# Two transformer blocks on one core: stacks of the even attention made earlier, first norm's squares added on VectorE, norm sums taken inside the last output tile

## Chip, cores, metric

One core of a Trainium2 chip runs the whole program in one launch. The metric is the device time in microseconds (us), lower is better. TensorE is called PE in the profile, VectorE DVE, ScalarE ACT, GpSimd POOL, and SyncE (which here only issues transfers) SP.

## The reference

Input x has 512 tokens of width 1024, the context 256 tokens. A first block of two layers modulates, mixes and projects; a second block of two layers adds attention, a gated unit and two feed-forward nets. Cut to what the change touches:

```python
def rms_norm(x, g):
    y = xf * lax.rsqrt(jnp.mean(xf * xf, axis=-1, keepdims=True) + EPS)
    return (y * g)

# first_block, layer l
mod_x = (silu_c @ w_mod[l] + b_mod[l])
sh_x, sc_x, g_x = jnp.split(mod_x, 3, axis=-1)
hx = rms_norm(x, norm_pre[l]) * (1.0 + sc_x) + sh_x       # the same for ctx
px = hx @ w_in
mx = mixer(px, pc)
x = x + g_x * rms_norm(mx @ w_out[l], norm_post[l])

# second_block, layer i
h = rms_norm_2(x, norm_mix_pre[i]); h = attention(h) or chunked_sgu(h)
x = x + rms_norm_2(h, norm_mix_post[i])
h = conv_gated_ffn(rms_norm_2(x, norm_ffn_pre[i]))
x = x + rms_norm_2(h, norm_ffn_post[i])
```

So there are twelve norms over the 1024 features: one before and one after each mixer or net.

## The kernel before

Features lie on the 128 partitions in KT = 8 tiles, tokens along the free axis (TX = 512 of x, TC = 256 of the context, TA both). All engines run their own hand-written order of instructions and meet through counting semaphores. There is no scheduler, so the code's order is the order of the work.

**Weights.** Every float32 matrix is read as panels of 1 MB (`load`, on SyncE) into a ring of RING = 3 slots `raw`. VectorE turns each into two float32r parts (`split_at`: a cast to `whi`, a subtraction to `wlo`, which takes raw's place). TensorE multiplies hi*hi, hi*lo and lo*hi (`mm3`, lines 385 to 387). `panel_done` frees the slot for the load three panels later.

**Start.** SyncE issues parameters, x, context and constants (`mats`), then the twelve modulation panels of layer 0 in six loads of 2 MB (`load_mod0`), among them the first two panels of the even phase. ScalarE squares one tile at a time (`square("pre0", kt)`), and TensorE sums each tile over its partitions by multiplying with a column of ones (`column_sums`, line 506, for pre0 and pre1 tile by tile: `sums_by_tile`). After that come the root (ScalarE, `norm_root`), its reciprocal (VectorE, `norm_inverse`) and its spread over the partitions (TensorE, `spread`, line 531). TensorE makes the modulation rows (`mod_panel`, line 490), ScalarE copies them out (`mod_row`), TensorE turns them into columns (`mod_columns`, line 499). VectorE then normalises x tile by tile (`pre_norm`), and the first panel of the even phase follows at its pace (`paced_panel`).

**Even attention.** 48 units: four pairs of heads (hp), six query tiles (t), two heads (a). For each pair, a stack of operands (query and key parts side by side on partitions) is made: ScalarE casts (`even_hi`), VectorE subtracts (`even_lo`, line 1786), and SyncE issues 24 small transfers in a row (`build_stack`, lines 349 to 351). The next pair's cast stands at unit (t, a) = (1, 1) of a pair, its subtraction at (2, 0). TensorE computes scores two units ahead (`even_scores`, line 630), which at a pair's first unit waits for the stack. VectorE takes maxima (line 1834) and mixes the two softmaxes (line 1852).

**Norms behind and ahead of panels.** For the ten other norms VectorE adds the squares of tiles 0 to 6 (`add_square`, line 1632), and `sums_added` on TensorE multiplies with ones twice: the sum `acc`, then the last square `sq[1]`. After an output projection (out0, out1, wo, the "long" ffn_out and sgu_out) this follows the last panel. For a norm ahead of a net (mixpre, ffnpre) the scale per token is applied after the matmul: `paced_pair` runs the first two panels, `sums_added` follows, then the third panel, then `spread`, after which ScalarE copies the spread root to `rxs` and VectorE scales the panels (`q_scaled`, `ff["scaled"]`), which frees their PSUM banks for the fourth panel.

Of the kernel before, what the change touches and what calls it, by code (L numbers as in the profile page):

```python
# [36 lines left out]
KT = D // P  # L37
# [51 lines left out]
def build_kernel(nc, dram, out):  # L89
    with ExitStack() as ctx:  # L90
# [145 lines left out]
        BY_TILE = {"pre0": 0, "pre1": 1}  # L236
        ADDED = {k: i for i, k in enumerate(k for k in NORMS if k not in BY_TILE)}
        ADDS = KT - 2

# [10 lines left out]
        n_full = {k: sem(f"{k}_full") for k in BY_TILE}  # L250
# [129 lines left out]
        def _(pe):  # L380
# [128 lines left out]

            def sums_by_tile(key, tiles):  # L510
# [233 lines left out]
            def out_projection(phase, norm, hi, lo, parts_made, kts=range(KT)):  # L744
                p0 = FIRST[phase]
                for k in range(4):
# [4 lines left out]
                    if k == 0:  # L751
                        paced_panel(p0, (0, 1), None, hi, lo, parts_made, kts)
                    else:
                        feature_panel(p0 + k, (2 * s, 2 * s + 1), None, hi, lo, kts)
# [15 lines left out]
            sums_added("post0")  # L770
# [173 lines left out]
            feature_panel(p0 + 3, (3, 4), None, o1hi, o1lo, kts1)  # L944
            pe.wait_ge(y_free, Y_AT["out1"] + 2)
            sums_added("post1")
# [86 lines left out]
            sums_added("mixpost0")  # L1033
# [1366 lines left out]
```

## Time and profile before

| | before |
|---|---|
| median of 3 runs | 2368.78 us (2367.3 to 2369.19) |
| the profiled execution's own time | 2371.67 us |
| its span, first to last instruction | 2369.9 us |
| PE / DVE / ACT busy | 2218.5 / 1345.8 / 545.0 us |
| granted TensorE clock, mean | 0.960 |

The profiled execution took 2.9 us more than the median. Its span leaves 1.8 us around it. Busy TensorE time counts matmuls, whose ends are modelled.

### The profile page before, as it was taken

The page shows a single profiled execution, that of the slowest core. Times are in us where ns is not written, and L with a number is a line of the kernel's source. Part 1 is how long each engine was busy: PE and PEld are TensorE (multiplying, and loading weights), DVE is VectorE, ACT ScalarE, POOL GpSimd, SP SyncE. Part 2 cuts the span into 40 slices and gives each one's busy share as a digit, 9 for nine tenths or more (in the row PEclk, how much of TensorE's full clock was granted, in tenths as well). Part 3 has the DMA queues.
Part 4 walks back from the last instruction along what each step waited for, and adds up shares of the span by engine and source line. Part 5 has one row for each costly group of instructions (what it writes and reads, how often), then busy time and mean ns, then how long its engine had stood idle before and what let it go on. Part 6 is the DMA issues. An engine that isn't in the chain of part 4 may idle for free.

```text
span 2369.9 us, 28220 instructions
## 1 busy us (share of the span) xinstructions
PE 2218.5 (94%) x11900; PEld 1819.0 (77%) x11900; DVE 1345.8 (57%) x1727; ACT 545.0 (23%) x1071; POOL 46.3 (2%) x31
## 2 busy tenths in 40 slices
PE   6999997779999989889899999999999999999997
PEld 5788885448878767777788888878888787788886
DVE  2323436884464264668578773464687436877633
ACT  2111014771231263246311111021100002211100
POOL 0000000000001020110000000000000000000000
PEclk9899998898899999899899999999999999999998
DMA  8022223121122110211223222322221222223222
GB/s 360 19 107 107 107 108 76 45 59 39 69 71 99 39 68 28 84 50 37 71 90 106 89 90 94 105 86 89 89 89 63 91 96 89 89 90 106 79 98 72
DMA packets 35246, 203.99 MB, mean 86 GB/s; under 512 B 4912, under 2 KB 5168, under 8 KB 17200
## 3 DMA queue, kind: packets, MB, share of 16 engines
q1 hardware_dynamic: 33744, 197.47, 24.1%
q10 hardware_dynamic: 1376, 4.72, 0.6%
q8 instruction: 94, 1.54, 0.3%
q14 instruction: 32, 0.26, 0.0%
HBM read 190.64 MB, written 2.10 MB: 81 GB/s over the span
## 4 chain that ended last, share of the span: by engine, by line
PE 86%; DVE 8%; SPq 2%; ACT 2%; issue 1%; DMA 1%; DVEq 0%; POOL 0%; POOLq 0%; ACTq 0%
PE ps L385 22%; PE ps L386 22%; PE ps L387 21%; PE ps L458 3%; PE ps L459 3%; PE ps L460 3%; PE ps L506 2%; PE ps L550 1%; DVE stat L1834 1%; PE ps L490 1%; PE ps L630 1%; PE ps L1120 1%; PE ps L531 1%; PE ps L851 1%; SPq L349 1%
## 5 line engine op out<-in xcount | busy, mean ns | idle before, releaser
L1623 DVE CAST whi<-raw 128x2048 fp32r<-128x2048 f32 (+2 forms) x162 | 184.4, 1138 | 485.7 <-DMA raw<-in_ffn_out 117.4
L385 PE MATMUL ps<-h2hi,whi 128*128 128x512 f32 x1040 | 410.2, 394 | 18.6 <-DVE h2lo L1720 12.2
L386 PE MATMUL ps<-h2lo,whi 128*128 128x512 f32 x1040 | 407.8, 392 | 0.0
L387 PE MATMUL ps<-h2hi,wlo 128*128 128x512 f32 x1040 | 407.6, 392 | 0.0
L1624 DVE TENSOR_TENSOR wlo<-raw,whi 128x2048 fp32r<-128x2048 f32 (+2 forms) x162 | 341.6, 2108 | 5.6
L385 PE MATMUL ps<-h1hi,whi 128*128 128x512 f32 (+1 forms) x768 | 274.5, 357 | 9.5 <-DVE h1lo L1665 8.3
L386 PE MATMUL ps<-h1lo,whi 128*128 128x512 f32 (+1 forms) x768 | 270.1, 352 | 0.0
L387 PE MATMUL ps<-h1hi,wlo 128*128 128x512 f32 (+1 forms) x768 | 268.2, 349 | 0.0
L385 PEld LDWEIGHTS ps<-h2hi,whi 128*128 128x128 f32 x1040 | 197.3, 190 | 61.1 <-issue 13.3
L387 PEld LDWEIGHTS ps<-h2hi,wlo 128*128 128x128 f32 x1040 | 197.1, 189 | 41.3
L386 PEld LDWEIGHTS ps<-h2lo,whi 128*128 128x128 f32 x1040 | 197.3, 190 | 40.6
L385 PE MATMUL ps<-mhi,whi 128*128 128x512 f32 x544 | 212.6, 391 | 6.6 <-DVE mlo L1643 3.9
L387 PE MATMUL ps<-mhi,wlo 128*128 128x512 f32 x544 | 212.4, 390 | 0.0
L386 PE MATMUL ps<-mlo,whi 128*128 128x512 f32 x544 | 212.3, 390 | 0.0
L385 PEld LDWEIGHTS ps<-h1hi,whi 128*128 128x128 f32 x768 | 147.8, 192 | 34.8 <-issue 10.4
L386 PEld LDWEIGHTS ps<-h1lo,whi 128*128 128x128 f32 x768 | 147.7, 192 | 19.8 <-issue 1.4
L387 PEld LDWEIGHTS ps<-h1hi,wlo 128*128 128x128 f32 x768 | 146.9, 191 | 19.9
L385 PEld LDWEIGHTS ps<-mhi,whi 128*128 128x128 f32 x544 | 102.5, 188 | 29.1 <-issue 4.3
L1144 ACT ACTIVATE temp<-ps 128x512 f32<-128x512 f32 (+1 forms) x48 | 25.5, 564 | 429.4 <-PE ps L387 413.6
L387 PEld LDWEIGHTS ps<-mhi,wlo 128*128 128x128 f32 x544 | 102.4, 188 | 21.4
L386 PEld LDWEIGHTS ps<-mlo,whi 128*128 128x128 f32 x544 | 102.5, 188 | 21.2
L2130 DVE TENSOR_TENSOR temp<-ps,rxs 128x1024 f32<-128x1024 f32 x44 | 53.9, 1224 | 89.3 <-PE ps L387 74.5
(284 smaller groups left out, 2993.9 us busy)
## 6 DMA issues: line engine op xcount, KB each, us to landing
raw<-in_ffn_in SPq DMA_DIRECT2D x44, 1024.0 KB, 4.9
raw<-in_ffn_out SPq DMA_DIRECT2D x32, 704.0 KB, 4.0
raw<-in_even SPq DMA_DIRECT2D x16, 1024.0 KB, 7.0
mod_w<-in_mod SPq DMA_DIRECT2D x6, 2048.0 KB, 26.0
mraw<-in_mod SPq DMA_DIRECT2D x12, 1024.0 KB, 4.9
raw<-in_odd SPq DMA_DIRECT2D x12, 1024.0 KB, 5.0
raw<-in_sgu_v SPq DMA_DIRECT2D x12, 1024.0 KB, 4.9
raw<-in_sgu_u SPq DMA_DIRECT2D x12, 1024.0 KB, 5.1
```

The lines of the kernel that those rows point to most:

```text
L349: sp.dma_start(q[to, :].bitcast(F32), (qhi, eql[:, hp, :])[part][rows, :].bitcast(F32)).then_inc(ea["stack"], 16)
L385: pe.matmul(o, r(lhi), r(rhi), start=first, stop=False, **kw)
L386: pe.matmul(o, r(lhi), r(rlo), start=False, stop=False, **kw)
L387: return pe.matmul(o, r(llo), r(rhi), start=False, stop=last, **kw)
L458: pe.matmul(o, lhi, rhi, start=kt == 0, stop=False)
L459: pe.matmul(o, lhi, rlo, start=False, stop=False)
L460: return pe.matmul(o, llo, rhi, start=False, stop=kt == KT - 1)
L506: done = pe.matmul(ps[:, 6, 48 + t:49 + t], tile[:, t * P:(t + 1) * P], ones[:, 0:1], start=first and t == tiles[0], stop=last, skip_group ...
L1144: return act.activation(o, in_, func, **kw)
L1623: step(dve.tensor_copy(whi[:, slot, 0:width].bitcast(F32R), raw[:, slot, 0:width]))
L1624: tell(dve.tensor_tensor(wlo[:, slot, 0:width].bitcast(F32R), raw[:, slot, 0:width], whi[:, slot, 0:width], ALU.subtract), split_done, n + 1)
L2130: tell(dve.tensor_tensor(gu[s], ps[:, b:b + 2, :], rxs[:].unsqueeze(1).broadcast_to([P, 2, TX]), ALU.mult), ff["scaled"], c0 + n + 1)
```

## The change

The diff touches four places.

1. Start: `mats` is loaded before x, and the even phase's first two panels go between the modulation loads. pre0's squares (x and context, 768 columns) are added on VectorE, and TensorE sums the total once, after the second modulation panel. `spread("pre0")` stands after the fifth. The second even panel's cast moves to ScalarE, at tile 4 of the first norm, and its subtraction behind that norm.
2. Even attention: the next pair's cast is made at unit (0, 0), the subtraction at (0, 1).
3. Norms ahead of nets: VectorE adds the eighth square too, TensorE sums only `acc` (`pre_sums`). `spread` goes between the two halves of the third panel (not so for mixpre1, where it stays).
4. Norms behind projections: the sum over `acc` is put into the last tile (`last_out_panel`, `long_out`), with only the last square's sum left behind it. In out1 and wo ScalarE can square tile 6 when the last panel's first half is done. VectorE's adds go ahead of the splits beside them.

In this diff the edit at mixpre0 stands for ffnpre0 and ffnpre1 too, `last_sums(norm)` with the test of (t, half) is in `long_out`, `cast_ahead` in ScalarE's `hi_parts`, and the last piece in `out_splits`.

```diff
             sp.dma_start(pc[:], dram["params"]).then_inc(params_in, 16)
+            sp.dma_start(mats[:], dram["mats"]).then_inc(params_in, 16)
             sp.dma_start(x[:], dram["xT"]).then_inc(x_in, 16)
             sp.dma_start(cx[:], dram["ctxT"]).then_inc(x_in, 16)
-            sp.dma_start(mats[:], dram["mats"]).then_inc(params_in, 16)
...
-            for i in range(4):
-                load_mod0(i)
-            for k in range(2):
-                load("even", k, k)
+            load_mod0(0)
+            load_mod0(1)
+            load("even", 0, 0)
+            load_mod0(2)
+            load_mod0(3)
+            load("even", 1, 1)
...
+            def last_out_panel(n, banks, hi, lo, norm, kts=range(KT)):
+                pe.wait_ge(split_done, n + 1)
+                for j in range(2):
+                    for i, kt in enumerate(kts):
+                        if (j, i) == (1, 4):
+                            acc_sums(norm)
+                        last = x_part(n, banks[j], j, kt, hi, lo, i == 0, i == KT - 1)
+                    if j == 0:
+                        last.then_inc(out_half, 1)
+                last.then_inc(panel_done, 1)
...
-            def sums_added(key):
-                pe.wait_ge(n_acc, ADDS * ADDED[key] + ADDS)
+            def acc_sums(key):
+                pe.wait_ge(n_acc, ADD_AT[key] + ADDS)
                 column_sums(acc, range(4), True, False)
+            def last_sums(key):
                 pe.wait_ge(n_sq, KT * NORM[key] + KT)
                 column_sums(sq[1], range(4), False, True).then_inc(n_mm, 1)
+            def pre_sums(key, tiles=range(4)):
+                pe.wait_ge(n_acc, ADD_AT[key] + KT - 1)
+                column_sums(acc, tiles, True, True).then_inc(n_mm, 1)
...
-            sums_by_tile("pre0", range(6))
-            mod_panel(0, 0)
-            spread("pre0", range(6))
             for k in range(8):
-                if k:
-                    mod_panel(0, k)
+                mod_panel(0, k)
+                if k == 2:
+                    pe.wait_ge(n_rt, 1)
                 if k:
                     mod_columns(0, k - 1)
+                if k == 1:
+                    pre_sums("pre0", range(6))
+                elif k == 4:
+                    spread("pre0", range(6))
...
-            sums_added("mixpre0")
-            feature_panel(p0 + 2, (4, 5), None, h2hi, h2lo)
-            spread("mixpre0", range(4))
+            pre_sums("mixpre0")
+            feature_panel(p0 + 2, (4, 5), None, h2hi, h2lo, between=lambda: spread("mixpre0", range(4)))
...
+                        if (t, half) == (KT - 1, 1):
+                            acc_sums(norm)
...
-                sums_added(norm)
+                last_sums(norm)
...
+                    if ctx_too and kt == 4:
+                        act.wait_ge(raw_loaded[1], 16)
+                        copy(whi[:, 1, :].bitcast(F32R), raw[:, 1, :]).then_inc(cast_ahead, 1)
...
-                if (t, a) == (1, 1) and hp < 3:
+                if (t, a) == (0, 0) and hp < 3:
                     even_hi(hp + 1)
...
-                if (t, a) == (2, 0) and hp < 3:
+                if (t, a) == (0, 1) and hp < 3:
                     even_lo(hp + 1)
...
+            for kt in range(1, KT):
+                add_square("pre0", kt, TA)
             norm_inverse("pre0", 6)
-            for n in range(2):
-                split_at(n)
+            split_at(0)
...
-                add_square(key, 6)
+                for kt in (4, 5, 6):
+                    add_square(key, kt)
+                split_at(p0 + 5)
```

On TensorE, at the program's start, the instructions stood so (L506 sums over partitions, L490 a modulation panel, L499 its columns, L531 the spread root):

```order
L506 MATMUL ps<-mats,temp 128x1 x48
L490 MATMUL ps<-mod_w_74,cs 32x256 x8
L531 MATMUL ps<-mats,root 128x128 x6
L490 MATMUL ps<-mod_w_74,cs 32x256 x8
L499 MATMUL ps<-pc,rows 128x2 x2
```

They now stand so (the same functions, at lines 511, 495, 504 and 556):

```order
L495 MATMUL ps<-mod_w_74,cs 32x256 x16
L504 MATMUL ps<-pc,rows 128x2 x2
L511 MATMUL ps<-mats,temp 128x1 x6
L495 MATMUL ps<-mod_w_74,cs 32x256 x8
L504 MATMUL ps<-pc,rows 128x2 x2
L495 MATMUL ps<-mod_w_74,cs 32x256 x8
L504 MATMUL ps<-pc,rows 128x2 x2
L495 MATMUL ps<-mod_w_74,cs 32x256 x8
L504 MATMUL ps<-pc,rows 128x2 x2
L556 MATMUL ps<-mats,root 128x128 x6
```

48 products with ones became 6, and the modulation panels no longer stand behind them.

On VectorE, in the first pair of the even attention, the subtraction (L1786) stood after the maximum (L1834) that follows unit 4's mix (L1852):

```order
L1852 SCALAR_TENSOR_TENSOR prob_87<-prob_87,stat 128x768
L1834 TENSOR_REDUCE stat<-ps 128x2
L1786 TENSOR_TENSOR eql<-eq,eql 128x768
L1786 TENSOR_TENSOR ekl<-ek,ekl 128x768
L1848 RECIPROCAL stat<-stat 128x1
L1849 SCALAR_TENSOR_TENSOR stat<-stat,lam 128x1
L1852 SCALAR_TENSOR_TENSOR temp<-temp,stat 128x768
```

It now stands three units earlier, behind unit 1 (maximum L1876, mix L1894, subtraction L1828):

```order
L1890 RECIPROCAL stat<-stat 128x1
L1891 SCALAR_TENSOR_TENSOR stat<-stat,lam 128x1
L1894 SCALAR_TENSOR_TENSOR prob_87<-prob_87,stat 128x768
L1876 TENSOR_REDUCE stat<-ps 128x2
L1828 TENSOR_TENSOR eql<-eq,eql 128x768
L1828 TENSOR_TENSOR ekl<-ek,ekl 128x768
```

The same instructions are there as before, so the work of a pair on VectorE is unchanged, and only SyncE's start on the next stack moves.

## Rows read from the trace of the kernel before

**Rows 1.** Waits of TensorE, whole span: total us, times, longest.

```profile
PE ps L630 <- DMA esb<-ekl: 17.5, 3, 6.2
```

**Rows 2.** Timeline of the first 60 us: start, duration, engine, line, count, idle.

```profile
14.72 1.28 ACT L1208 ACT_TABLE_LOAD   x1
16.02 0.42 ACT L1144 ACTIVATE temp<-ctx 128x256 f32<-128x256 f32 x1
16.46 0.63 ACT L1144 ACTIVATE temp<-x 128x512 f32<-128x512 f32 x1
...
17.24 20.61 PE L506 MATMUL ps<-mats,temp 128*128 128x1 f32 x96 [17.24 <-ACT temp L1144]
...
37.78 1.93 PE L490 MATMUL ps<-mod_w,cs 128*32 128x256 f32 x16
...
42.35 1.07 PE L490 MATMUL ps<-mod_w,cs 128*32 128x256 f32 x16
...
54.57 0.38 DVE L1749 TENSOR_TENSOR modc<-ps,pc 128x16 f32<-128x16 f32 x2 [8.92 <-PE ps L499]
...
59.14 0.77 PE L385 MATMUL ps<-h1hi,whi 128*128 128x512 f32 x1 [4.68 <-DVE h1lo L1665]
```

**Rows 3.** Timeline of 97 to 112 us, modulation panels 8 to 11, one row.

```profile
105.09 1.01 PE L499 MATMUL ps<-pc,rows 128*128 128x2 f32 x4 [0.50 <-ACT rows L1144]
```

**Rows 4.** Loads issued at 1.70, 4.38 and 5.92 us: KB, us to landing.

```profile
ctx<-in_ctxT SPq DMA_DIRECT2D x1, 1024.0 KB, 10.3
...
mod_w<-in_mod SPq DMA_DIRECT2D x1, 2048.0 KB, 28.1
...
raw<-in_even SPq DMA_DIRECT2D x1, 1024.0 KB, 31.6
```

**Rows 5.** Timeline of even attention, VectorE and the DMA queue of SyncE.

```profile
397.36 0.95 DVE L1786 TENSOR_TENSOR eql<-eq,eql 128x768 fp32r<-128x768 f32 x1
...
399.21 0.51 SPq L349 DMA_DIRECT2D whi<-eql  x1
...
414.64 0.59 SPq L351 DMA_DIRECT2D esb<-ekl  x1
...
418.56 1.76 DVE L1834 TENSOR_REDUCE stat<-ps 128x2 f32<-128x1536 f32 x1 [5.71 <-PE ps L630]
...
459.92 1.76 DVE L1834 TENSOR_REDUCE stat<-ps 128x2 f32<-128x1536 f32 x1 [2.38 <-PE ps L630]
...
501.29 1.76 DVE L1834 TENSOR_REDUCE stat<-ps 128x2 f32<-128x1536 f32 x1 [5.22 <-PE ps L630]
```

**Rows 6.** Timeline after two pre norms: qkv (995 on) and ffn0_in (1190 on).

```profile
998.15 2.37 DVE L1624 TENSOR_TENSOR wlo<-raw,whi 128x2048 fp32r<-128x2048 f32 x1
...
1003.36 1.84 PE L506 MATMUL ps<-mats,temp 128*128 128x1 f32 x16
...
1008.41 2.29 DVE L1624 TENSOR_TENSOR wlo<-raw,whi 128x2048 fp32r<-128x2048 f32 x1
...
1016.08 1.05 PE L531 MATMUL ps<-mats,root 128*128 128x128 f32 x8
...
1019.41 0.50 PE L385 MATMUL ps<-h2hi,whi 128*128 128x512 f32 x1 [2.29 <-DVE sq L2038]
...
1209.82 0.50 PE L385 MATMUL ps<-h2hi,whi 128*128 128x512 f32 x1 [2.06 <-DVE temp L2130]
```

**Rows 7.** Timeline at the ends of out1, wo and ffn0_out.

```profile
969.62 2.69 PE L506 MATMUL ps<-mats,temp 128*128 128x1 f32 x16 [1.57 <-DVE temp L1632]
972.35 0.27 ACT L1144 ACTIVATE root<-ps,eps 128x4 f32<-128x4 f32 x1 [2.27 <-PE ps L506]
...
1162.52 0.27 ACT L1144 ACTIVATE root<-ps,eps 128x4 f32<-128x4 f32 x1 [1.26 <-PE ps L506]
...
1538.33 0.60 ACT L1144 ACTIVATE temp<-ps 128x512 f32<-128x512 f32 x1 [13.88 <-PE ps L387]
...
1540.07 0.26 ACT L1144 ACTIVATE root<-ps,eps 128x4 f32<-128x4 f32 x1 [0.66 <-PE ps L506]
```

More of the change, by code:

```diff
@@ L235, in build_kernel @@
         NORM = {k: i for i, k in enumerate(NORMS)}
-        BY_TILE = {"pre0": 0, "pre1": 1}
-        ADDED = {k: i for i, k in enumerate(k for k in NORMS if k not in BY_TILE)}
+        BY_TILE = {"pre1": 0}
         ADDS = KT - 2
+        ADDED = {k: 0 if k == "pre1" else KT - 1 if "pre" in k else ADDS for k in NORMS}
+        ADD_AT = {k: sum(ADDED[j] for j in NORMS[:i]) for i, k in enumerate(NORMS)}
         n_sq = sem("norm_squares")
@@ L249, in build_kernel @@
         out0_x = sem("out0_last_x")
-        n_full = {k: sem(f"{k}_full") for k in BY_TILE}
+        out_half = sem("out_last_half")
+        cast_ahead = sem("second_panel_cast")
+        n_full = {k: sem(f"{k}_full") for k in ("pre0", "pre1")}
         n_hi = {k: sem(f"{k}_hi") for k in NORMS if "pre" in k}
@@ L752, in out_projection @@
                         paced_panel(p0, (0, 1), None, hi, lo, parts_made, kts)
+                    elif k < 3:
+                        feature_panel(p0 + k, (2 * s, 2 * s + 1), None, hi, lo, kts)
                     else:
-                        feature_panel(p0 + k, (2 * s, 2 * s + 1), None, hi, lo, kts)
+                        last_out_panel(p0 + k, (2 * s, 2 * s + 1), hi, lo, norm, kts)
             pe.wait_ge(y_free, Y_AT["out0"] + 1)
@@ L769, in _ @@
                 ctx_part(p0 + 3, 5, 0, kt, h1hi, h1lo, i == 0, i == KT - 1)
-            sums_added("post0")
+            acc_sums("post0")
+            last_sums("post0")
             for i, kt in enumerate(kts0):
@@ L943, in _ @@
             pe.wait_ge(n_sq, KT * NORM["post1"] + 2)
-            feature_panel(p0 + 3, (3, 4), None, o1hi, o1lo, kts1)
+            last_out_panel(p0 + 3, (3, 4), o1hi, o1lo, "post1", kts1)
             pe.wait_ge(y_free, Y_AT["out1"] + 2)
-            sums_added("post1")
+            last_sums("post1")
             spread("post1", range(4))
@@ L1038, in ffn @@
                 paced_pair(p0, h2hi, h2lo, n_ok[f"ffnpre{layer}"])
-                sums_added(f"ffnpre{layer}")
-                feature_panel(p0 + 2, (4, 5), None, h2hi, h2lo)
-                spread(f"ffnpre{layer}", range(4))
+                pre_sums(f"ffnpre{layer}")
+                feature_panel(p0 + 2, (4, 5), None, h2hi, h2lo,
+                              between=lambda: spread(f"ffnpre{layer}", range(4)))
                 for n in range(3, 22):
@@ L1210, in _ @@
                 if kt >= 2:
-                    act.wait_ge(n_tile, kt - 1)
+                    act.wait_ge(n_acc, ADD_AT["pre0"] + max(1, kt - 2))
                 step(copy(sq[kt % 2][:, TX:TA], cx[:, kt, :], ACT.Square))
                 square("pre0", kt, x[:, kt, :])
-            norm_root("pre0", range(6))
             for k in range(8):
                 mod_row(0, k)
+                if k == 1:
+                    norm_root("pre0", range(6))
             hi_parts("pre0", h1hi, 0, True)
@@ L1341, in out_copy @@
                     n, b = FIRST[phase] + k, banks[k]
-                    act.wait_ge(panel_done, n + 1)
                     for j in range(2):
+                        if k == 3 and j == 0:
+                            act.wait_ge(out_half, 1 if phase == "out1" else 2)
+                        else:
+                            act.wait_ge(panel_done, n + 1)
                         kw = dict(bias=par(bias, 2 * k + j)) if bias else {}
@@ L1631, in add_square @@
                 a, b = (sq[0], sq[1]) if kt == 1 else (acc, sq[kt % 2])
-                tell(dve.tensor_tensor(acc[:, 0:TX], a[:, 0:TX], b[:, 0:TX], ALU.add), n_acc, ADDS * ADDED[key] + kt)
+                tell(dve.tensor_tensor(acc[:, 0:n_tok], a[:, 0:n_tok], b[:, 0:n_tok], ALU.add), n_acc, ADD_AT[key] + kt)
             def add_ctx_square(i, kt):
@@ L1733, in post_then_scaled @@
                 low(KT - 1)
+                add_square(pre, KT - 1)
             step(dve.memset(eps[:], EPS))
@@ L1765, in _ @@
                      lambda kt, c: modc[0][:, kt, c:c + 1])
+            dve.wait_ge(cast_ahead, 1)
+            tell(dve.tensor_tensor(wlo[:, 1, :].bitcast(F32R), raw[:, 1, :], whi[:, 1, :], ALU.subtract), split_done, 2)
             for n in range(2, 4):
@@ L2011, in out_splits @@
                 p0 = FIRST[phase]
-                for k in range(4):
+                for k in range(3):
                     split_at(p0 + k + 2)
-                    for kt in ((), (1,), (2, 3), (4, 5))[k]:
+                    for kt in ((), (1,), (2, 3))[k]:
                         add_square(key, kt)
-                add_square(key, 6)
+                for kt in (4, 5, 6):
+                    add_square(key, kt)
+                split_at(p0 + 5)
             out_splits("out1", "post1")
```

10 lines of the change are left out of this document (5 added, 5 removed).

## The prediction, made blind

> **What bounds the kernel now.** I read the page's busy times first: TensorE is busy for 2218.5 us of a span of 2369.9 (the table above), so what counts is the 150 us in which it is not, and the time in which it does work that could be left out. The waits of TensorE name one large releaser among the stages that the diff touches: three waits for the stacks' transfers, 17.5 us [rows 1]. The timeline of the start shows 17.24 us of nothing and then 20.61 us of sums over partitions, before the modulation's first panel at 37.78 [rows 2]. The rest of the change touches small gaps, each read from its timeline [rows 6, 7].
>
> **1. The start.** Now: the squares begin at 16.02, the 96 rows of sums (48 products, two rows each) take 20.61 us, 0.215 a row, the panels end so that VectorE can start the modulation at 54.57, and the paced panel starts at 59.14 [rows 2]. All this is one chain, so what the last modulation column gains, the kernel gains. New chain: x and context have landed at about 12.7 (the context came at 1.70 + 10.3 = 12.0 with `mats` behind it [rows 4]; the bytes ahead are now the same). The table load of 1.28 follows, so squares start at 14.0, not 16.02. A tile costs ScalarE 0.42 + 0.63, and VectorE an add of 768 columns, which is priced by the 0.95 us of a subtraction of that width [rows 2, 5]. Both run side by side, 1.07 a tile: squares end at 22.5, adds at 23.5. ScalarE's first row copy stands behind the squares, so panel 1 can only start at 22.9. It takes 1.93 at the lower clock level [rows 2] and ends at 24.8. Columns of 1.01 follow [rows 3], to 25.8, and then 6 products (12 rows of 0.215), to 28.4. An iteration of panel and columns without a gap costs 2.9 at this level: three of them (k = 2, 3, 4) end at 37.1. The spread takes 2.7 (42.35 - 37.78 - 1.93 [rows 2]), to 39.8. Panel 5 ends at 41.7. Panels 6 and 7 need the fourth modulation load. It landed at 4.38 + 28.1 = 32.5 and now has 1 MB ahead of it. Two MB took 37.5 - 32.5 = 5.0 us (to the second even panel, at 5.92 + 31.6) [rows 4], so it lands at 35.0 and is not waited for.
>
> What remains depends on the clock. The granted clock reads full in these stretches, but the same 16 panel rows take 1.93 at 37.78 and 1.07 at 42.35 [rows 2]: the first is the 1.2 GHz level, the second 2.4. The 20 us of one-column sums did not raise it. The panel of 1.93 and the spread after it, back to back, did. In the new order spread and panel 5 are the same pair of neighbours, so I take the upper level from 41.7 on: an iteration then costs (54.57 - 42.35) / 7 = 1.75 [rows 2], two of them with the leftover columns 4.7. The end is at 46.4, a gain of 54.57 - 46.4 = **8.2**. Bounds: all at the lower level, 41.7 + 1.0 + 2 x 2.9 + 1.0 = 49.5, gain 5.1; the upper level from panel 2 on, about 41, gain 13.5. I take the middle because panels 8 to 11, separated by gaps of 0.50, stayed at the lower level [rows 3].
>
> The Trainium skill ("TensorE: Matmul & The Clock Gate", Part 1) says that the throttled clock is the default and that sustained activity releases it. This speaks against the change, which empties TensorE's first 20 us, and would give 5.1 in place of 8.2, a sum of 28.2, if the loop does not count as sustained. The trace agrees only in part: the busy time taken away did not raise the clock.
>
> The cast that moved to ScalarE: 128x256 takes 0.42 and 128x512 0.63 [rows 2], so 2048 columns cost 0.42 + 7 x 0.21 = 1.9, and four times 0.63 = 2.5 at most. VectorE's pace in the norm is two products and two subtractions of x and context a tile, ScalarE's only two casts, so a delay of 2 us is taken up by a tile of lead. Value: nothing; uncovered 1 us. Panel 1's subtraction (below 2.37 [rows 6]) goes behind the norm, where TensorE still has the last tile and eight context products to do. Value: nothing; uncovered 2 us.
>
> **2. The stacks.** The subtraction at 397.36 is followed by 24 issues from 399.21 to 414.64, and the last lands 2 us later. Scores start then, and VectorE's maximum at 418.56 after 5.71 us idle. The other two boundaries cost VectorE 2.38 and 5.22 [rows 5]. TensorE's waits add to 17.5, but VectorE is what the units run at, so its idle time is the price: 13.3 in all. The second is smaller because a weight split of VectorE fills the wait. With the subtraction three units of some 3 us earlier, the stack is there 9 us earlier, against waits of at most 6.2 [rows 1]. ScalarE's cast and VectorE's two subtractions are the same work in another unit. SyncE's wait for the scores of the pair before holds for pair 2 and 3, but those are done one pair earlier. Gain **13.3**. Bounds: 10 if cast and subtraction at a boundary uncover 1 us each time; 16.5 if the short idles around the boundaries go too.
>
> **3. Sums ahead of nets.** Four norms lose half of their 16 rows (1.84 a norm, so 0.85 to 0.92 [rows 6]): **3.4**. VectorE's extra add (under 0.95) delays the third panel's split, which ended at 998.15 + 2.37 = 1000.5, while TensorE comes to it at 1005.2 [rows 6]: hidden by 4 us. Uncovered it would cost 0.7 each.
>
> **4. The spread in mid-panel.** After the spread TensorE waited 2.29 us for the first scaling at qkv and 2.06 at ffn0_in [rows 6], and ffn1_in has the same code. Spread, root copy and scaling took from 1016.08 to 1019.4, 3.4 us. Half a panel is 5.5 us ((1016.08 - 1005.1) / 2). So all three waits go: **6.4**. Bounds: 0 if the split of the fourth panel, which stands ahead of the scaling on VectorE, ended later than the panel; in the trace it ended at 1008.41 + 2.29 = 1010.7, before 1016.08 [rows 6]. I take 6.4, and 4 as the low end.
>
> **5. Sums behind projections.** In out1 the sums began 1.57 us after the last matmul, ran cold for 2.69, and the root came at 972.35 [rows 7]. New: 0.85 more in the tile, one square instead of two and no add behind it, 8 rows: the root at about 970.6, gain 1.7. In wo two biased copies stand between the last square and the root on ScalarE, which was idle for only 1.26 before the root at 1162.52. Square and copies now start 0.85 later less one square of 0.6, so 1.0 could come through; I take 0.85 [rows 7]. In the long ones there is nothing to gain: the first 8 rows ran in the shadow of the last square (1538.33, 0.60), and the root came at 1540.07 [rows 7]. Put into the tile, they lengthen it by 0.85 and the root comes at 1540.9. Three of these: -2.5. Sum **0.0**; from -2 to +1.5. Out0 has its sums where it had them.
>
> **Sum.** 8.2 + 13.3 + 3.4 + 6.4 + 0.0 = 31.3. The profiled execution's 2371.67 (span 2369.9 and 1.8 around it) would become 2340.4. It lay 2.9 above the median, so the median of 2368.78 becomes **2337.5**.
>
> **Rivals.**
> - *The clock stays low through the start.* Gain 28, time 2340.5. For it: panels 8 to 11 [rows 3]. The page of the Trainium skill named above, "TensorE: Matmul & The Clock Gate", would give this one. Against it: panel and spread raised it once.
> - *The upper level comes early in the loop.* Gain 36.5, time 2332. For it: there are no gaps in the new loop. Against: two thirds of it is panel work.
> - *ScalarE or TensorE becomes the bound at pair boundaries*, so that only half of the stacks' gain arrives. Gain 24.5, time 2344. For it: ScalarE gets 1.6 us of casts just where scores, maxima and exps of heavy units follow light ones. Against: VectorE is the one without gaps around 397 to 405.
> - *The stacks don't come earlier*, since SyncE issues them behind something else. Gain 18, time 2351. Against: each stack's other conditions are met before the cast.
> - *Slower than before.* TensorE enters the even panels from an emptier start. If the paced panel (a tile each 2.4 us) does not bring the upper level and the full panels behind it stay at 1.2 GHz, each costs its own length more: 11.0 for x [rows 6] and half of that for the context, 16.5. From the second such panel on, the 31 us are gone: 2370 with two, 2387 with three. For it: the kernel starts with less work. Against: the paced panel starts after 4.68 us of idleness now too [rows 2] and rose within it.
>
> **Chances.** Forecast 0.55 (its own range 2333 to 2341), clock low 0.18, clock early 0.09, half the stacks 0.11, no stacks 0.03, slower 0.02, and 0.02 for something that leaves no change. The range 2330 to 2345 leaves out the last three, and part of the others' tails. Faster by over 0.2% (about 5 us, what a measurement of this kernel can tell from no change): 0.96; within 0.2%: 0.02; slower: 0.02.
>
> **What would show it.** Modulation columns ending near 46 instead of 54.5, with 16 panel rows going from 1.93 to 1.07 after the spread. No wait of TensorE for the stacks, and no idle time of VectorE over 1 us at boundaries; the stage from the first maximum to the last unit shorter by 13. Eight rows of sums, not 16, and no wait for the first scaling in qkv and both ffn_in. Roots of the long projections 0.8 later after the tile's last but one matmul. Wrong would make it: a wait for `norm_added` inside a last tile, a wait of panel 1 for its split, a fourth panel that waits for its own split.

## The result, and the profile after

The changed kernel runs in **2327.46 us** (median of four runs, 2325.4 to 2330.14) against 2368.16 us for the kernel before (four runs, 2367.3 to 2369.19): ratio 0.9829, 95% interval 0.9812 to 0.9846. It is faster by 40.7 us, where the prediction said 31.3 and put the lower end of its range at 2330. The direction and three of the four parts came as forecast; the size is 9 us off, and what follows is mainly about these 9 us.

The profiled execution took 2330.14 us, span 2328.4. The start first: TensorE's timeline of the changed kernel (start, duration, operation, count, idle time before with its releaser), which answers to [rows 2].

```profile
25.49 1.93 PE L495 MATMUL ps<-mod_w,cs 128*32 128x256 f32 x16 [4.26 <-ACT rows L1175]
27.36 1.01 PE L504 MATMUL ps<-pc,rows 128*128 128x2 f32 x4
28.23 2.70 PE L511 MATMUL ps<-mats,temp 128*128 128x1 f32 x12
...
39.21 2.91 PE L556 MATMUL ps<-mats,root 128*128 128x128 f32 x12
42.05 1.84 PE L495 MATMUL ps<-mod_w,cs 128*32 128x256 f32 x16
43.81 0.61 PE L504 MATMUL ps<-pc,rows 128*128 128x2 f32 x4
44.49 1.07 PE L495 MATMUL ps<-mod_w,cs 128*32 128x256 f32 x16
...
52.99 0.77 PE L390 MATMUL ps<-h1hi,whi 128*128 128x512 f32 x1 [4.67 <-DVE h1lo L1703]
```

The loop has no gaps, the 96 rows of sums are 12, and the level rose where the forecast put it: panel 5 at 42.05 still took 1.84, panel 6 took 1.07. VectorE began the modulation at 48.42 instead of 54.57, 6.15 earlier and not 8.2. The missing 2 us lie ahead of the loop, in ScalarE's timeline:

```profile
14.20 1.28 ACT L1242 ACT_TABLE_LOAD   x1 [7.39 <-DMA ctx<-in_ctxT]
15.49 0.42 ACT L1175 ACTIVATE temp<-ctx 128x256 f32<-128x256 f32 x1
...
18.66 0.42 ACT L1175 ACTIVATE temp<-ctx 128x256 f32<-128x256 f32 x1 [1.12 <-DVE temp L1670]
```

The context landed at 14.2, not at 12.7 as worked out from [rows 4]; squares began at 15.49, not 14.0. Another 1.1 us went at the third tile, where ScalarE waited for VectorE's first add; the forecast had both run side by side without a wait. So panel 1 began at 25.49, not 22.9. The landing is the execution's and not the edit's: in the nine profiles of kernels that have this start, with the table load behind the wait for the context, that load began between 12.33 and 14.48 us (fill_norms and front_alone, both below), and in start_alone at 12.50.

In the attention, the queue's and VectorE's timelines answer to [rows 5]. The second pair's 24 issues went out between these two rows:

```profile
381.95 0.51 SPq L354 DMA_DIRECT2D whi<-eql  x1
...
397.35 0.59 SPq L356 DMA_DIRECT2D esb<-ekl  x1
```

and the first maximum of the heavy units behind them had waited 0.18 us, for a matmul, where it had waited 5.71 for the stack:

```profile
410.67 1.76 DVE L1876 TENSOR_REDUCE stat<-ps 128x2 f32<-128x1536 f32 x1 [0.18 <-PE ps L657]
```

TensorE's waits name no stack any more (17.5 us in [rows 1]). The lead grows from 6.03 to 20.17 us over the attention: 14.1 for a forecast of 13.3.

Behind out1 the changed kernel's TensorE shows sums, spread, the pre norm's sums and the spread in mid-panel (before: [rows 6, 7]):

```profile
940.37 0.95 PE L511 MATMUL ps<-mats,temp 128*128 128x1 f32 x8
...
944.97 1.02 PE L511 MATMUL ps<-mats,temp 128*128 128x1 f32 x8 [0.78 <-ACT temp L1175]
946.63 1.16 PE L556 MATMUL ps<-mats,root 128*128 128x128 f32 x8 [0.64 <-DVE root L1686]
...
975.19 0.95 PE L511 MATMUL ps<-mats,temp 128*128 128x1 f32 x8
...
981.57 1.05 PE L556 MATMUL ps<-mats,root 128*128 128x128 f32 x8
982.37 0.48 PE L390 MATMUL ps<-h2hi,whi 128*128 128x512 f32 x1
```

The wait of 2.29 for the first scaling is gone. But two rows are shorter than the change made them. The spread is the same eight rows as before and took 1.16, not 2.08 (972.95 in the trace of before), and from it to the pre norm's sums it is 28.56 us (946.63 to 975.19), not 30.41 (972.95 to 1003.36), though TensorE's work between them was not edited. The granted clock from the spread to the sums was 0.88, against 0.81 before.

Lead by stage, in the two profiled executions: start 6.0; attention +14.1; out0 and pre1, where nothing was edited, +4.2; out1's root +1.9; its paced pair +2.8; the sums and spread of qkv +2.6; wo with ffn0_in +6.2; ffn0_out, mixpre1 and sgu +0.1; sgu_out with ffn1_in +3.6; ffn1_out -0.9. So the excess over the forecast is 4.2 in a stage that is not edited, some 6 in the norms from out1 on and 0.8 in the attention, less 2 at the start.

### The profile page after: what moved, and what is told of

Its sections match the earlier page's. It is cut to its first block, busy times and chain, and to the rows that moved or that the text cites. A ratio compares the mean times of both kernels' runs of the same rounds, so it can differ in the third digit from the quotient of the medians.

```text
span 2328.4 us, 28021 instructions
## 1 busy us (share of the span) xinstructions
PE 2192.0 (94%) x11784; PEld 1790.3 (77%) x11784; DVE 1354.2 (58%) x1737; ACT 546.2 (23%) x1072; POOL 47.6 (2%) x31
## 4 chain that ended last, share of the span: by engine, by line
PE 86%; DVE 9%; ACT 2%; issue 1%; DMA 1%; SPq 0%; DVEq 0%; POOL 0%; POOLq 0%; ACTq 0%
PE ps L390 22%; PE ps L391 22%; PE ps L392 22%; PE ps L463 3%; PE ps L464 3%; PE ps L465 3%; PE ps L575 2%; PE ps L511 1%; DVE stat L1876 1%; PE ps L495 1%; PE ps L657 1%; PE ps L881 1%; PE ps L1151 1%; PE ps L556 1%; DVE prob L1894 1%
## 5 line engine op out<-in xcount | busy, mean ns | idle before, releaser
L392 PEld LDWEIGHTS ps<-h2hi,wlo 128*128 128x128 f32 x1040 | 196.4, 189 | 41.4
L390 PEld LDWEIGHTS ps<-mhi,whi 128*128 128x128 f32 x544 | 102.5, 188 | 29.0 <-issue 4.3
```

The source lines that it names most:

```text
L390: pe.matmul(o, r(lhi), r(rhi), start=first, stop=False, **kw)
L392: return pe.matmul(o, r(llo), r(rhi), start=False, stop=last, **kw)
```

## The experiments

The expectations name theories. CHAIN says that only removed waits and work count; CLOCK says that TensorE, beyond that, stays at 2.4 GHz or comes back to it sooner. Later ones say what they mean.

All were compared with the kernel before on the same chip. Over all these comparisons the kernel before ran 53 times: 2360.55 to 2373.31 us, mean 2366.8. "Mean" below is the mean of a kernel's runs, and +- the standard error of a difference; "clock" is the mean granted clock over the span, averaged over the runs.

### What the clock alone does

The 53 runs of before are the first result. They differ by 12.8 us with the same code, and the clock orders them: the four fastest (2360.55 to 2361.97) have 0.965 or 0.966, the four slowest (2371.89 to 2373.31) 0.959 or 0.960. A line through all 53 gives 1.5 us for each 0.001. It holds between executions of one code. Carried over to the difference of two kernels, as is done below, it gives an estimate and no proof; fill_norms below departs from it. The execution of before that I had read (2371.67, 0.960) was near the slow end.

Two profiled executions show it in a stretch with identical instructions, the odd attention and the first panels of out1. First the kernel before, then the changed one (its second profile, label after_again); columns are window, length, busy time of each engine with counts, granted clock, DMA share, GB/s.

```profile
828.30:931.20 102.90, 92.15 (x856) 66.87 (x855) 63.81 (x122) 56.71 (x110) 17.85 (x7) 0.95 0.15 52
```

```profile
800.60:899.60 99.00, 88.05 (x856) 63.98 (x855) 63.58 (x123) 56.80 (x110) 17.88 (x7) 1.00 0.16 54
```

856 matmuls in both, clock 0.95 against 1.00, 3.9 us apart. In the first profile of the changed kernel the same stretch took 102.5 us at 0.95, so this is the execution and not the edit.

The Trainium skill ("TensorE: Matmul & The Clock Gate", Part 1) says that the number of slow products at the start of one and the same kernel differs from run to run, with the phase of the gate. The traces agree that one code's clock differs from run to run, and here far behind the start too (the changed kernel's 0.95 and 1.00 in this stretch); no run shows the gate's phase.

### Each part alone

Four kernels: before with one part of the diff.

```diff
 stacks_alone
-                if (t, a) == (1, 1) and hp < 3:
+                if (t, a) == (0, 0) and hp < 3:
                     even_hi(hp + 1)
 (and even_lo at (0, 1) in place of (2, 0))
 start_alone: the hunks on loads, the modulation loop, pre0 and the cast ahead
 pre_alone
-            sums_added("mixpre0")
-            feature_panel(p0 + 2, (4, 5), None, h2hi, h2lo)
-            spread("mixpre0", range(4))
+            pre_sums("mixpre0")
+            feature_panel(p0 + 2, (4, 5), None, h2hi, h2lo, between=lambda: spread("mixpre0", range(4)))
 (and the same in ffn0, ffn1, mixpre1's sums)
 post_alone
-            feature_panel(p0 + 3, (3, 4), None, o1hi, o1lo, kts1)
+            last_out_panel(p0 + 3, (3, 4), o1hi, o1lo, "post1", kts1)
 (and the same in wo; acc_sums inside the last tile of long_out)
```

> The kernel before with the stacks' casts and subtractions at the pair's first units and nothing else. By rows of the trace after, the attention itself gave 14.1 us of lead. Theory CLOCK (the 9.4 us that I had not priced come from TensorE staying at 2.4 GHz or coming back to it sooner) leaves open whether out0's further 4.2 us hang on this part: 14 to 18 us faster than before, 2350 to 2354. Theory CHAIN (only removed waits and work count): 14.1 faster, 2354. Under 10 faster would say that the stacks need the other parts.

> The kernel before with the new start alone (loads reordered, first norm's squares added on VectorE, sums and spread between the modulation's panels, second panel's cast on ScalarE). CHAIN: the 6.2 us that the modulation columns came earlier in the trace after, 2362. CLOCK: the same 6.2, unless a stage 600 us later depends on when it runs: then out0's 4.2 show up here, 2358.

> The kernel before with the pre norms' part alone (mixpre0, ffnpre0, mixpre1, ffnpre1: the last square added too, 8 rows of sums, the spread inside the next tile); post norms as before. CLOCK: the excess of the paced pairs belongs to the post norms' sums ahead of them, so this gives its price, 3.4 + 6.4 = 9.8 us less, 2358. CHAIN: the excess of 5.3 us at the three paced pairs belongs to the shorter pre norms, so 15 us less, 2353.

> The kernel before with the post norms' part alone (out1, wo and the three long projections: added squares summed inside the last tile, four products after it). CHAIN: priced at 0.0 (+1.7, +0.85, three times -0.85), 2368. CLOCK: TensorE goes on into spread and paced pair at the upper level more often, some 5 us more: 2363.

| part | median (runs) | ratio, 95% interval | mean less before's | clock | forecast |
|---|---|---|---|---|---|
| stacks | 2352.05 (4) | 0.9947, 0.9927 to 0.9967 | -13.2 +- 1.9 | 0.963 | -13.3 |
| start | 2356.48 (10) | 0.9968, 0.9956 to 0.9980 | -8.8 +- 1.1 | 0.9635 | -8.2 |
| pre norms | 2357.07 (7) | 0.9962, 0.9946 to 0.9978 | -9.4 +- 1.7 | 0.962 | -9.8 |
| post norms | 2362.07 (10) | 0.9985, 0.9974 to 0.9997 | -3.6 +- 1.1 | 0.967 | 0.0 |

(Before on that chip: median 2364.78, mean 2365.5, clock 0.963, 22 runs.) Three parts came at their price, at a clock within 0.001 of before's. So pre_alone speaks for CLOCK (9.8) and against CHAIN, which gave the pre norms 15. The post part was priced at nothing and was 3.6 us faster, and its clock is 0.004 higher, which by the line above is 6 us, more than it gained. Nothing was edited between the inverses of post0's and pre1's roots, yet that stage took 22.65 us in the profile of before and 21.04 in that of post_alone. Over all profiled executions without fills in it, it lies between 20.98 and 22.75: chance again, not a part.

Where the post part gains can be read more sharply than from whole times. From the root behind out1, wo, ffn0_out and sgu_out to the root of the next pre norm it changes no instruction. ScalarE's roots at ffn0_out and at the pre norm behind it, before and in post_alone (the first row of before, at 1540.07, is in [rows 7]):

```profile
1572.45 0.26 ACT L1144 ACTIVATE root<-ps,eps 128x4 f32<-128x4 f32 x1 [8.64 <-PE ps L506]
```

```profile
1529.56 0.26 ACT L1175 ACTIVATE root<-ps,eps 128x4 f32<-128x4 f32 x1 [0.65 <-PE ps L509]
...
1560.49 0.26 ACT L1175 ACTIVATE root<-ps,eps 128x4 f32<-128x4 f32 x1 [8.12 <-PE ps L509]
```

That is 32.38 against 30.93 us. The four stretches together, in every kernel without fills or doubled sums there (one profile each, the changed kernel's two):

| | pre norms as before | pre norms changed |
|---|---|---|
| post norms as before | 130.5 to 131.1 (before, stacks_alone, start_alone, front_alone) | 126.9, 127.0 (pre_alone, post_undone) |
| post norms changed | 126.0, 126.1 (pre_undone, post_alone) | 122.5 to 123.6 (after, after_again, nets_alone, fill_start) |

On average 4.7 us hang on the post part in the left column and 4.0 in the right, with the same work. At a single place chance still has its say: the spread behind out1, 2.08 in the trace of before and 1.16 in the changed kernel, took 1.16 in stacks_alone too.

start_alone also says how far the forecast of the clock in the start can be trusted. Its TensorE, with the same code as the changed kernel's start:

```profile
37.52 2.91 PE L556 MATMUL ps<-mats,root 128*128 128x128 f32 x12
40.35 1.94 PE L495 MATMUL ps<-mod_w,cs 128*32 128x256 f32 x16
42.22 1.02 PE L504 MATMUL ps<-pc,rows 128*128 128x2 f32 x4
43.17 1.93 PE L495 MATMUL ps<-mod_w,cs 128*32 128x256 f32 x16
45.03 1.01 PE L504 MATMUL ps<-pc,rows 128*128 128x2 f32 x4
45.97 1.93 PE L495 MATMUL ps<-mod_w,cs 128*32 128x256 f32 x16
```

Here the level never rose. Of the twelve profiled starts with this loop it rose by the second panel behind the spread in nine, and not behind the spread in three: this one, fill_start and sums_twice. The last two have other work ahead of the loop or in it, so start_alone is the one case in ten with the loop as in the changed kernel.

### The changed kernel again, and parts taken out of it

```diff
 after_again: no edit
 post_undone (out1, wo and the long projections)
-            last_out_panel(p0 + 3, (3, 4), o1hi, o1lo, "post1", kts1)
+            feature_panel(p0 + 3, (3, 4), None, o1hi, o1lo, kts1)
-            last_sums("post1")
+            acc_sums("post1")
+            last_sums("post1")
 pre_undone (qkv, both ffn_in, mixpre1)
-            pre_sums("mixpre0")
-            feature_panel(p0 + 2, (4, 5), None, h2hi, h2lo, between=lambda: spread("mixpre0", range(4)))
+            acc_sums("mixpre0")
+            last_sums("mixpre0")
+            feature_panel(p0 + 2, (4, 5), None, h2hi, h2lo)
+            spread("mixpre0", range(4))
 front_alone: before with start and stacks; nets_alone: before with pre and post norms
```

> The changed kernel once more, against more runs of the kernel before. The four parts alone gave -12.7, -8.3, -7.7 and -2.7, in all -31.4, and in two of them stages that they don't touch were up to 4.5 us shorter than in the one profiled execution of before. Theory CHANCE: where TensorE's clock falls differs from execution to execution of the same code, by up to 11 us over 22 runs of before, and the first comparison had only four runs of each; then the difference over more runs is the sum of the parts, 30 to 34 us, some 2332 to 2335. Theory TOGETHER: the parts joined raise the clock beyond each alone: 38 to 41 us again, 2325 to 2327.

> The changed kernel with its post norms' sums as they were before (16 rows behind the tile in out1, wo and the long projections). The post part alone was 3.6 us faster than before as a mean of ten runs. ADDITIVE: 3 to 4 us slower than the changed kernel, 2330. TOGETHER (in the changed kernel the paced pairs behind these sums keep the clock only if the sums are short): 7 to 9 slower, 2335. PRICE (clock left out): 0.

> The changed kernel with the pre norms as before (16 rows of sums, the spread behind the third panel with its wait for the first scaling). ADDITIVE: the 9.4 us slower that the part alone gained over before, 2336. TOGETHER: 12 or more slower, 2339. PRICE: 9.8 slower.

> The kernel before with the start and the stacks' part, norms behind the attention as before. Against before: ADDITIVE: 8.8 + 13.2 = 22.0 us less, 2344 to 2346. TOGETHER inside this pair: 27 less, 2340. PRICE: 8.2 + 13.3 = 21.5 less.

> The kernel before with the pre norms' and the post norms' part, start and stacks as before. Against before: ADDITIVE: 9.4 + 3.6 = 13.0 us less, 2354. TOGETHER inside this pair (the shorter sums on both sides of the same paced pairs keep the clock up there): 18 less, 2349. PRICE: 9.8 less.

| kernel | median (runs) | ratio, 95% interval | mean less before's | clock |
|---|---|---|---|---|
| after_again | 2326.22 (4) | 0.9820, 0.9800 to 0.9840 | -42.4 +- 1.5 | 0.969 |
| post_undone | 2331.37 (4) | 0.9855, 0.9834 to 0.9876 | -35.5 +- 2.0 | 0.964 |
| pre_undone | 2343.82 (6) | 0.9894, 0.9875 to 0.9914 | -25.2 +- 2.2 | 0.966 |
| front_alone | 2344.25 (4) | 0.9901, 0.9888 to 0.9913 | -23.4 +- 1.2 | 0.965 |
| nets_alone | 2351.79 (6) | 0.9934, 0.9922 to 0.9947 | -15.4 +- 1.2 | 0.965 |

CHANCE said that the first comparison was lucky, ADDITIVE that the parts add up, TOGETHER that joined they raise the clock beyond each alone, PRICE that only the forecast's terms count. front_alone came as ADDITIVE and PRICE had it (22.0 and 21.5; TOGETHER 27). nets_alone at 15.4 +- 1.2 lies between 13.0 and 18.

CHANCE falls as an account of the whole excess: against nine further runs of before the changed kernel gained 42 us again, not 30 to 34. Its eight runs have mean 2326.7 and clock 0.968, before's 53 runs 2366.8 and 0.9625. The difference of clock is 0.0058, worth 8.6 us by before's own line, which leaves 31.5 of 40.1 us. The forecast without a change of clock was 31.3. That the two agree so closely is partly luck, for the line is an estimate here.

Without the post part the changed kernel's mean is 2332.3, 5.6 us slower than 2326.7 (+- 1.9), and its clock 0.9642 against 0.9684, by the line 6.2 us. So the post part's work is worth about nothing, as priced, and by the line its clock about 6; the four stretches above give it 4.0. The place, in post_undone's timeline of out1:

```profile
938.04 2.68 PE L511 MATMUL ps<-mats,temp 128*128 128x1 f32 x16 [1.57 <-DVE temp L1666]
941.37 2.08 PE L556 MATMUL ps<-mats,root 128*128 128x128 f32 x8 [0.64 <-DVE root L1682]
...
971.76 0.95 PE L511 MATMUL ps<-mats,temp 128*128 128x1 f32 x8
```

It is the picture of before again: cold sums, cold spread, 30.39 us to the pre norm's sums, where the changed kernel needs 28.56.

Taking the pre part out costs 15.9 us, not 9.8 (TOGETHER had said 12 or more); 0.0024 of clock is 3.5 of it. One place where the clock enters is the removed wait itself, in pre_undone behind the third panel of qkv:

```profile
991.02 1.05 PE L556 MATMUL ps<-mats,root 128*128 128x128 f32 x8
994.36 0.50 PE L390 MATMUL ps<-h2hi,whi 128*128 128x512 f32 x1 [2.29 <-DVE sq L2085]
994.71 0.40 PE L391 MATMUL ps<-h2lo,whi 128*128 128x512 f32 x1
...
995.65 0.47 PE L392 MATMUL ps<-h2hi,wlo 128*128 128x512 f32 x1
995.92 0.63 PE L390 MATMUL ps<-h2hi,whi 128*128 128x512 f32 x1
```

The same 2.29 as in [rows 6], but here products fell from 0.40 to 0.63 us afterwards; in the profile of before they stayed at 0.40. The wait costs 2.29 and, in some executions, a stretch at 1.2 GHz behind it.

Do the parts help each other? Alone they sum to 35.0 +- 3.8 (one set of before's runs serves all four, so its error counts four times), the pairs to 38.8 +- 1.9, the whole is 41.4 +- 1.0 (both comparisons, each with before's runs on its own chip). The pairs are short of the whole by little more than the error of the difference, the single parts by 1.6 of it. TOGETHER may be true for a few us; it is not shown.

### Work in the waits, and sums twice

If the clock is the cause, useless products in TensorE's waits must pay, and more narrow products must cost more than their rows.

```diff
+            def filler(bank, count):
+                for _ in range(count):
+                    pe.matmul(ps[:, bank, 0:P], ident, ident, start=True, stop=True)
 fill_norms (out1; wo and the long projections alike)
+            pe.wait_ge(y_free, Y_AT["out1"] + 3)
+            filler(0, 2)
             last_sums("post1")
+            filler(0, 2)
             spread("post1", range(4))
+            filler(0, 10)
 fill_start
+            filler(2, 24)
             for k in range(8):
                 mod_panel(0, k)
+                if k == 0:
+                    filler(2, 8)
 ...
             mod_columns(0, 7)
+            filler(2, 9)
 sums_twice (pre_sums)
+                column_sums(acc, tiles, True, True)
                 column_sums(acc, tiles, True, True).then_inc(n_mm, 1)
```

> The changed kernel with products of 128x128 in TensorE's waits at the five post norms ahead of h2 nets (two behind the last tile, two behind the sums, ten behind the spread), into bank 0. CLOCK: the stretches at the lower level behind out1, wo and the three long projections (6.8, 6.8, 10.2, 6.8 us in the record of the profiled execution) go, each worth 1 to 2 us: 3 to 7 us faster than the changed kernel. CHAIN: 0, or 1 slower.

> The changed kernel with TensorE kept at work through the start: 24 products of 128x128 ahead of the first modulation panel, 8 behind it, 9 behind the last column, in time in which it waits, into a bank that nothing else uses then. CLOCK: the loop of panels, columns, sums and spread then runs at 2.4 GHz from its beginning (panel 1.07 and columns 0.61 in place of 1.93 and 1.01): 5 to 7 us faster than the changed kernel. CHAIN: nothing hangs on these products, 0; up to 2 slower if one of the fills outlasts its wait.

> The changed kernel with the sums of pre0, mixpre0, ffnpre0, mixpre1 and ffnpre1 issued twice (the second overwrites the first), so 8 rows more in each, 12 in pre0. CHAIN: 4 times 0.85 at the upper level and 2.6 at pre0, 6.0 slower than the changed kernel. CLOCK: the double sums also let the clock fall in more executions, 8 or more slower.

fill_norms: 2321.51 (five runs, 2319.16 to 2326.62), ratio 0.9808, 0.9787 to 0.9829; clock 0.9746; mean 2322.2, 4.5 +- 1.5 below the changed kernel's. CHAIN, which said 0 or 1 slower, falls. The line would make 9 us of the 0.006 of clock. One reading, not tested, is that a higher level in a wait counts in the mean and gains nothing. Its TensorE at out1:

```profile
937.64 0.60 PE L580 MATMUL ps<-mats 128*128 128x128 f32 x4
938.49 1.05 PE L511 MATMUL ps<-mats,temp 128*128 128x1 f32 x8 [0.24 <-ACT temp L1193]
939.41 0.69 PE L580 MATMUL ps<-mats 128*128 128x128 f32 x4
940.18 1.16 PE L556 MATMUL ps<-mats,root 128*128 128x128 f32 x8
941.17 2.40 PE L580 MATMUL ps<-mats 128*128 128x128 f32 x20
...
967.54 0.95 PE L511 MATMUL ps<-mats,temp 128*128 128x1 f32 x8
```

From spread to the pre norm's sums it is 27.36 us now, and the four stretches of the table above add up to 117.2. The three kernels side by side, 40 us around this place, each from its own trace (post_undone, after_again, fill_norms): granted clock 0.83, 0.91, 1.00.

```profile
926.00:966.00 40.00, 33.74 (x142) 27.89 (x141) 29.25 (x40) 14.45 (x23) 0.45 (x1) 0.83 0.15 53
```

```profile
924.00:964.00 40.00, 34.53 (x155) 28.37 (x154) 31.71 (x42) 15.57 (x25) 0.92 (x1) 0.91 0.16 53
```

```profile
924.00:964.00 40.00, 37.86 (x190) 31.50 (x189) 31.52 (x42) 15.75 (x25) 0.56 (x1) 1.00 0.15 53
```

sums_twice: 2337.29 (five runs, 2333.86 to 2343.78), ratio 0.9872, 0.9850 to 0.9893; clock 0.966. Its mean is 11.4 us above the changed kernel's for rows worth 6.0; 0.0024 less clock accounts for 3.5 more. CLOCK had said 8 or more.

fill_start: 2322.96 (four runs), ratio 0.9807, 0.9787 to 0.9828; mean 2322.9, 3.8 faster than the changed kernel where 5 to 7 were expected, and not in the way expected. Its mean clock, 0.9655, can't be set beside the others': the record of its clock reads 1.2 GHz for 27.3 us from 25.8 on, while after_again's reads full there, though its panels took 1.93 as well.

```profile
18.19 1.26 PE L495 MATMUL ps<-mod_w,cs 128*32 128x256 f32 x16 [3.22 <-DMA mod_w<-in_mod]
19.38 3.46 PE L580 MATMUL ps<-mats 128*128 128x128 f32 x16
24.49 1.07 PE L495 MATMUL ps<-mod_w,cs 128*32 128x256 f32 x16 [1.65 <-ACT rows L1184]
25.49 0.80 PE L504 MATMUL ps<-pc,rows 128*128 128x2 f32 x4
26.15 2.70 PE L511 MATMUL ps<-mats,temp 128*128 128x1 f32 x12
28.78 1.93 PE L495 MATMUL ps<-mod_w,cs 128*32 128x256 f32 x16
...
49.18 4.11 PE L580 MATMUL ps<-mats 128*128 128x128 f32 x18
53.99 0.47 PE L390 MATMUL ps<-h1hi,whi 128*128 128x512 f32 x1 [0.71 <-DVE h1lo L1712]
```

The fills raised the level for panels 0 and 1, and the loop lost it again at once and stayed at 1.93 a panel to its end, though it has no gap. Modulation began at 49.42, later than in after_again (48.34). What was won lies behind the last fill: the even panels begin with a product of 0.47, not 0.77, and the kernel is 1.7 us ahead of after_again when the modulation's last columns are added (101.04 against 102.71).

### More fills

fill_more has the fills of fill_norms, with fourteen products behind the spread where that had ten, and the last fill of the start, and adds products between modulation panels 8 to 11 and their columns, three between the tiles of pre1's sums, and the second table load ahead of the wait for x. fill_more_long also has the long projections' first eight rows behind the tile again. fill_chosen is fill_more_long without pre1's fills.

```diff
 fill_more
                         last.then_inc(n_tile, 1)
+                        filler(0, 3)
 ...
+            act.preload_act_table(ACT.Sqrt)
             act.wait_ge(x_in, 32)
-            act.preload_act_table(ACT.Sqrt)
 fill_more_long, fill_chosen (long_out)
-                        if (t, half) == (KT - 1, 1):
-                            acc_sums(norm)
 ...
+                acc_sums(norm)
                 last_sums(norm)
```

> The changed kernel with products of 128x128 in more of TensorE's waits: the five post norms (two, two and fourteen), behind the start's last column (nine), between modulation panels 8 to 11 and their columns (three, then one each), between the tiles of pre1's sums (three each); and the second table load ahead of the wait for x. CLOCK: the fills at the post norms alone gave 4 to 5 us, the start's end some 2, the table load 1.3, pre1 1 to 3: 8 to 11 us faster than the changed kernel, 2316 to 2319. CHAIN: only the table load counts, 1.3 faster than the changed kernel.

> The kernel of the run before, and the long projections' first eight rows of sums behind the last tile again, as in the kernel before. PRICE: 0.85 us in each of three tiles back, 2.5 faster than the run before. CLOCK: if the sixteen rows behind the tile let the clock fall, 0 to 4 slower than it.

> The kernel fill_more_long without the fills between the tiles of pre1's sums. In the profile of fill_more each of these tiles took 2.99 us against 1.71 without fills, and the stretch between the inverses of post0 and pre1 31.0 us against 21.0. CLOCK with the path read from that profile: 9 us faster than fill_more_long, 2314. If that stretch was long by chance of the clock and not by the fills: 2322 again.

fill_more: 2325.74 (four runs, 2321.05 to 2330.82), ratio 0.9823, 0.9802 to 0.9844, where 2316 to 2319 had been expected: no better than the changed kernel despite a clock of 0.9745. Its TensorE in pre1, and below it after_again's:

```profile
603.79 1.63 PE L581 MATMUL ps<-mats 128*128 128x128 f32 x6
605.21 1.71 PE L511 MATMUL ps<-mats,temp 128*128 128x1 f32 x8
606.78 1.63 PE L581 MATMUL ps<-mats 128*128 128x128 f32 x6
```

```profile
609.66 12.91 PE L511 MATMUL ps<-mats,temp 128*128 128x1 f32 x64 [1.07 <-ACT temp L1175]
```

The eight tiles of sums already fill their stretch with narrow rows (64 in 12.91 us). They are the chain there, the fills stand in it at the lower level, and a tile takes 2.99 us instead of 1.6 or 1.7; the whole stage from post0's inverse to pre1's took 30.95 us, 22.74 in fill_chosen. A high clock share bought with work on the path is worth nothing.

fill_more_long: 2322.69 (four runs), ratio 0.9811, 0.9793 to 0.9828; its mean is 3.0 +- 2.6 below fill_more's at nearly the same clock, which agrees with the price of 2.5 but hardly tests it.

fill_chosen: **2316.7** (four runs, 2315.03 to 2318.75), ratio 0.9786, 0.9773 to 0.9798, clock 0.974. It is 10 us faster than the changed kernel and 6 faster than fill_more_long, where 9 (2314) had been expected. Of the 10 us, some 1.3 belong to the table load (1.28 long), which no longer stands behind the wait for x.

## Why the prediction missed

- **Start.** Forecast 8.2; 6.15 in the profile, 8.8 +- 1.1 in start_alone. The loop came as described. Squares were 1.5 us late in this execution because the context landed later, which varies by 2 us from one to the next, and ScalarE's wait of 1.1 for the first add was not in the sum. The clock's rise behind the spread is not a rule: three starts of twelve had none, one of them with the start unchanged. The rival with the low clock was real, and the 8.2 held in part by luck.
- **Stacks.** Forecast 13.3; 14.1 in the profile, 13.2 +- 1.9 alone. Right, by the mechanism given: VectorE's idle time, not TensorE's wait, was the price.
- **Pre norms.** Forecast 3.4 + 6.4 = 9.8; 9.4 +- 1.7 alone, 15.9 +- 2.1 taken out of the changed kernel. Waits and rows went as said.
- **Post norms.** Forecast 0.0. By the work this was nearly right: the long roots came 0.94 later each, for 0.85, the roots of out1 and wo 1.5 and 1.0 earlier, for 1.7 and 0.85, together -0.3. But the part is worth 3.6 us alone and 5.6 when it is taken out. **This is the term that failed**, in the step "In the long ones there is nothing to gain" and in pricing out1 and wo by their roots alone. I asked when the root comes and not in what state TensorE goes on. With the 16 narrow rows behind the projection, more of the spread and the paced pair ran at 1.2 GHz than with eight: the four stretches take 4.0 to 4.7 us more for the same work. A sign of it was in [rows 7], where the 16 rows took 2.69 us, not 1.84 as in [rows 6]; but two of the six profiles with these rows at out1 show 2.7, the others 1.92.
- **The sum.** All terms used durations of one execution and left its clock as it was. I named the clock as a cause in the start and, as a loss, in the even panels, but gave no case in which fewer narrow rows and shorter waits raise it elsewhere. By before's line that case is 8.6 of the 40.1 us; shown by runs are the post part's 3.6 to 5.6 of them. I also took the distance of the profiled execution to the median of three runs, 2.9; over 53 runs it is 4.4. The forecast of the time, 2337.5, was taken from the median, so this does not enter it.

Open stays where the other 3 to 5 us of the excess come from, and whether the parts joined raise the clock beyond the sum of the parts (6 us of means, at 1.6 standard errors). What makes the level fall behind 16 rows and less often behind eight is not shown either, only that it does.

## What to carry to other kernels

Price a removed wait or a removed run of narrow products twice: once by its rows, and once by what TensorE does next, since products behind it may run at half the clock. Read the same rows at several places: where one form takes 1.16 here and 2.08 there, the clock is part of the price. Compare kernels by several runs and look at the mean clock of each, for it warns of a change of clock beside the change of work; where the same instructions stand in both kernels, compare their stretches, which are less noisy than whole times. And before any filler goes in, ask whether the wait it fills is a wait: beside the path it gave 4.5 us, on the path it took it back.

## What was not expected of the hardware

- One kernel's time follows its mean granted clock: 53 runs between 0.959 and 0.966 lie between 2373.31 and 2360.55 us, about 1.5 us for each 0.001. The line did not carry over to a kernel with fills: 0.006 more gave 4.5 us, not 9.
- TensorE busy without a gap did not always keep 2.4 GHz: in fill_start the gapless loop of panels (1.07), columns and one-column sums fell back to 1.93 a panel within one round. In the changed kernel the last two panels with their columns, behind the spread, ran at 1.07.
- After a wait of 2.29 us products of pre_undone first ran at 0.40 us and only a microsecond later at 0.63; in the trace of before, behind the same wait, they stayed at 0.40.
